# Expert stage: whole 8 KB weight rows, 512-column up products, blocks overlapped on TensorE, at least two blocks an expert

## The chip, the cores and the metric

The kernel runs on one core of a Trainium2 chip. The metric is the device time of one execution in microseconds (us). Engines are called as in the profile: PE (TensorE), DVE (VectorE), ACT (ScalarE), POOL (GpSimd), SP (SyncE, which issues most DMAs).

## The reference, cut to what matters

The program computes a transformer block with a mixer and a mixture of experts, then two further layers, and a last norm, for 512 tokens of width 1024 in float32. The change lies in the mixture of experts: 32 experts, each token goes to 4, and each expert multiplies its tokens by a 1024 x 2048 matrix, applies a gated unit and multiplies by a 1024 x 1024 matrix.

```python
def moe(h, router_w, router_b, w_up, b_up, w_down, b_down):
    logits = (xt @ router_w + router_b).astype(jnp.float32)
    top_vals, top_idx = lax.top_k(logits, TOP_K)
    gates = jax.nn.softmax(top_vals, axis=-1)
    ...
    def expert_block(args):
        e, xb = args
        hu = xb @ w_up[e] + b_up[e]
        g = jnp.minimum(hu[:, :D_FF], SWIGLU_LIMIT)
        lin = jnp.clip(hu[:, D_FF:], -SWIGLU_LIMIT, SWIGLU_LIMIT)
        glu = g * jax.nn.sigmoid(SWIGLU_ALPHA * g)
        return ((lin + 1.0) * glu) @ w_down[e] + b_down[e]
    y_rows = lax.map(expert_block, (blk_expert, x_rows)).reshape(n_rows, d)
    y = jax.ops.segment_sum(y_rows * row_gate[:, None].astype(y_rows.dtype), row_tok, num_segments=t + 1)[:t]
```

## The kernel before, in words

**Blocks.** `route_stages` ranks the token-expert pairs on the device and fills three lists of 97 columns (`MAXB + 1`): which token rows a block takes, where its results go, and its gates. A block is 32 rows (`BR`) of one expert; an expert has its count of rows divided by 32, rounded up, and at least one block. The number of blocks is known only on the device: every engine reads `first_block` and runs its loop over the blocks.

**Rows.** A row of 1024 lies as four pieces of 256 on four groups of 32 partitions (`PARTS`), so a block fills 128 partitions. Since the left operand has 32 columns, four products run beside each other on the four column groups of PE, one for each quarter of the output columns.

**Weights.** An expert has 12 chunks of 1 MB: 8 up chunks, each two DMAs of 512 KB whose contiguous runs are 512 columns (2 KB), and 4 down chunks, one DMA with runs of 1024 columns (4 KB). 21 chunk buffers (`LENT`) are used in turn, a chunk being loaded into the buffer of the one 21 before it, so that SP (line 1832 on) waits for PE to have used that one in the last block of its expert. At most four chunks are in flight (`ahead`). The chunks of expert 0 and four of expert 1 are loaded in the routing stage.

**A block before.** PE (line 1940 on): seven up chunks, the transpose of the first half of the hidden units (line 1917), the eighth up chunk, two down chunks, the transpose of the second half, then the wait for the gather and the transposes of the next block's rows (line 1896), then two down chunks. Up products (line 1909) have 256 columns in two banks, one for each half of the hidden units. DVE adds the bias (2002), clamps (2004, 2005), multiplies (2007, 2009) with ACT's sigmoid (1972); ACT copies the transposes (1974, 1964). When the down products are done, DVE adds the bias (2012) and scales (2017) to give y.

**Gather and scatter.** POOL runs one loop (line 1878): once block b's rows are turned it issues the gather of b+1 (1865, an indirect DMA of 128 pieces of 1 KB) and then, once y is ready, the scatter of b (1873, an indirect DMA that adds y to x in memory). Instructions of one engine stay in their order, so a gather stands behind the scatter ahead of it:

```python
pool.wait_ge(rows_turned, b + 1)
gather(b + 1, b * 2 + 3)
pool.wait_ge(y_stored, b * 16 + 16)
pool.sem_inc(y_free, 1)
scatter(b, b * 2 + 4, b + 2)
```

There is one buffer for the gathered rows, one for y. The biases of an expert come on SP's queue and are spread over the partitions by line 1995.

## Time and profile before

| | |
|---|---|
| median of 3 runs | 3347.1 us (3343.88 to 3348.02) |
| profiled execution, its span | 3352.8 us |
| PE busy | 2825.7 us (84%) |
| DVE, ACT, POOL busy | 1291.4, 898.9, 280.1 us |
| expert stage, first to last product | 588.7 to 1738.5 us |
| bytes moved in the whole program | 581.92 MB |

The span runs from the first to the last instruction. The page cuts it into 40 slices of 83.8 us; PEclk is the clock granted to PE in tenths of 2.4 GHz. A float32 product shows as two records of the profile for each product of the program. A DMA's time to landing runs from its issue to its last semaphore update. SP's 512 KB DMAs share a semaphore, so the profile gives no landing for them.

### The profile page before, as it was taken

The numbers are of one execution on the slowest core, as the hardware profiler recorded it, in microseconds if no ns is written. First come the engines' busy times: TensorE is split into PE (matmuls) and PEld (weight loads), VectorE is DVE, ScalarE is ACT, GpSimd is POOL, SyncE is SP. The second block draws the span as 40 slices with busy tenths as digits, with TensorE's granted clock in tenths as the row PEclk, the third lists the DMA queues.
The fourth block names the chain that finished last, engine by engine and source line by source line (L and its number), as shares of the span: only waits on it lengthen the run. The fifth ranks groups of instructions, "written<-read, shape, count | busy, mean of one in ns | idle before, by whom it ended". The sixth has DMA issues, their size and how long they took to land. (4 is left out here: it accounts for less than half of the span.)

```text
span 3352.8 us, 65854 instructions
## 1 busy us (share of the span) xinstructions
PE 2825.7 (84%) x25476; PEld 2041.8 (61%) x25477; DVE 1291.4 (39%) x2922; ACT 898.9 (27%) x1856; POOL 280.1 (8%) x365
## 2 busy tenths in 40 slices
PE   6987675888888867989969597899999688899998
PEld 4965475444444423545538475778887566778886
DVE  1236554223222212333323474444443365643343
ACT  2233321112121101222213143343332133532232
POOL 1000000122221211222210100000000100000000
PEclk7996676899999967999989698999999788899999
DMA  6243006899999999799972300022221210022221
GB/s 181 77 154 117 1 13 252 318 385 344 382 386 387 344 391 388 241 353 386 361 260 84 96 1 26 26 76 101 101 101 60 69 51 1 26 73 85 95 101 50
DMA packets 299974, 581.92 MB, mean 174 GB/s; under 512 B 35780, under 2 KB 74372, under 8 KB 299764
## 3 DMA queue, kind: packets, MB, share of 16 engines
q1 hardware_dynamic: 279876, 557.27, 45.5%
q0 software_dynamic: 15792, 21.34, 2.9%
q8 instruction: 137, 2.24, 0.3%
q10 hardware_dynamic: 4098, 0.49, 0.1%
q14 instruction: 71, 0.58, 0.1%
HBM read 562.25 MB, written 16.78 MB: 173 GB/s over the span
## 5 line engine op out<-in xcount | busy, mean ns | idle before, releaser
L1909 PE MATMUL moe_up<-expert_w,mod 128*32 128x256 f32 x3856 | 243.1, 397 | 24.1 <-DMA expert_w<-in_exp_w_up 18.2
L1909 PE MATMUL moe_up<-ring,mod 128*32 128x256 f32 x3184 | 200.7, 402 | 30.9 <-issue 19.2
L1972 ACT ACTIVATE mod<-mod 128x128 f32<-128x128 f32 x158 | 48.9, 310 | 637.8 <-DVE mod L2004 637.8
L360 PE MATMUL mlp_bank<-hT_hi,mlp_w 128*128 128x512 f32 x512 | 199.4, 390 | 0.0
L362 PE MATMUL mlp_bank<-hT_hi,mlp_w 128*128 128x512 f32 x512 | 199.2, 389 | 0.0
L361 PE MATMUL mlp_bank<-hT_lo,mlp_w 128*128 128x512 f32 x512 | 199.2, 389 | 0.0
L360 PE MATMUL mlp_bank<-mlp_w,mlp_u_hi 128*128 128x512 f32 x512 | 199.2, 389 | 0.0
L361 PE MATMUL mlp_bank<-mlp_w,mlp_u_hi 128*128 128x512 f32 x512 | 199.2, 389 | 0.0
L362 PE MATMUL mlp_bank<-mlp_w,mlp_u_lo 128*128 128x512 f32 x512 | 199.2, 389 | 0.0
L1909 PEld LDWEIGHTS moe_up<-expert_w,mod 128*32 128x32 f32 x3856 | 122.7, 113 | 120.7 <-issue 27.1
L2002 DVE TENSOR_TENSOR mod<-moe_up,mod 128x256 f32<-128x256 f32 x158 | 67.1, 425 | 320.8 <-PE moe_up L1909 317.6
L402 ACT ACTIVATE mlp_w<-ring 128x1024 fp32r<-128x1024 f32 x128 | 125.1, 1053 | 207.8 <-PE mlp_bank L362 207.8
L1873 POOL DMA_INDIRECT mixed_rows<-mod,moe_place x80 | 128.3, 1604 | 544.2 <-DVE mod L2017 523.1
L1909 PEld LDWEIGHTS moe_up<-ring,mod 128*32 128x32 f32 x3184 | 104.2, 115 | 112.2 <-issue 46.0
L411 DVE TENSOR_TENSOR mlp_w<-ring,mlp_w 128x1024 fp32r<-128x1024 f32 x128 | 148.1, 1220 | 6.4 <-ACT mlp_w L402 6.4
L2012 DVE TENSOR_TENSOR mod<-moe_down,mod 128x256 f32<-128x256 f32 x79 | 33.6, 425 | 283.2 <-PE moe_down L1931 283.2
L1931 PE MATMUL moe_down<-expert_w,mod 128*32 128x256 f32 x2064 | 131.8, 393 | 1.7 <-DMA expert_w<-in_exp_w_down 0.4
L1508 DVE TENSOR_TENSOR x<-x,mlp_bank 128x512 f32<-128x512 f32 x64 | 43.9, 687 | 222.3 <-PE mlp_bank L362 222.3
L2427 DVE TENSOR_TENSOR mlp_relu<-mlp_relu 128x512 f32<-128x512 f32 x64 | 44.2, 691 | 191.2 <-ACT mlp_u_hi L2424 191.2
L360 PEld LDWEIGHTS mlp_bank<-hT_hi,mlp_w 128*128 128x128 f32 x512 | 96.1, 188 | 20.5 <-DVE hT_lo L671 0.4
L362 PEld LDWEIGHTS mlp_bank<-hT_hi,mlp_w 128*128 128x128 f32 x512 | 96.1, 188 | 20.1
L362 PEld LDWEIGHTS mlp_bank<-mlp_w,mlp_u_lo 128*128 128x128 f32 x512 | 96.1, 188 | 20.1
(522 smaller groups left out, 5765.1 us busy)
## 6 DMA issues: line engine op xcount, KB each, us to landing
expert_w<-in_exp_w_up SPq DMA_DIRECT2D x194, 512.0 KB
ring<-in_exp_w_up SPq DMA_DIRECT2D x150, 512.0 KB
ring<-in_w_ff SPq DMA_DIRECT2D x32, 2048.0 KB, 8.7
expert_w<-in_exp_w_down SPq DMA_DIRECT2D x47, 1024.0 KB, 11.1
ring<-in_exp_w_down SPq DMA_DIRECT2D x39, 1024.0 KB, 10.8
moe_w<-in_exp_w_up SPq DMA_DIRECT2D x74, 512.0 KB
ring<-in_ada_w SPq DMA_DIRECT2D x12, 2048.0 KB, 11.9
hT<-in_exp_w_up SPq DMA_DIRECT2D x48, 512.0 KB
```

The source lines that it names most:

```text
L360: nc.tensor.matmul(out, lhsT.hi, rhs.hi, start=(i == 0), stop=False)
L361: nc.tensor.matmul(out, lhsT.hi, rhs.lo, start=False, stop=False)
L362: mm = nc.tensor.matmul(out, lhsT.lo, rhs.hi, start=False, stop=last)
L402: nc.scalar.activation(halves.hi[:, at], w[:, at], ACT.Copy).then_inc(hi_made, 1)
L411: nc.vector.tensor_tensor(halves.lo[:, at], w[:, at], halves.hi[:, at].bitcast(F32), ALU.subtract).then_inc(lo_made, 1)
L1508: return nc.vector.tensor_tensor(k.x[:, t, cols], k.x[:, t, cols], psum, ALU.add)
L1873: pool.indirect_dma_start(x_parts, bass.IndirectOffsetOnAxis(ap=place[:], axis=0), y, None, compute_op=op).then_inc(y_stored, 16)
L1909: mm = nc.tensor.matmul(up[half][quarter[q], 0:2 * UNITS], rowsT[:, f % 2, quarter[f // 2]], chunk[r][c][:, :, j, q * UNITS:(q + 1) * UNIT ...
L1931: mm = nc.tensor.matmul(down[quarter[q], 0:YCOLS], hidT[:, half, quarter[f]], chunk[r][c][:, j, q * YCOLS:(q + 1) * YCOLS], start=(half == ...
L1972: nc.scalar.activation(sig[:, half], pre[:, half, 0:UNITS], ACT.Sigmoid, scale=ALPHA).then_inc(sig_ready, 1)
L2002: nc.vector.tensor_tensor(pre[:, half], up[half][:, 0:2 * UNITS], bias[:, 2 * half * UNITS:2 * (half + 1) * UNITS], ALU.add).then_inc(up_t ...
L2427: chain(nc.vector.tensor_tensor(r, r, r, ALU.mult))
```

## The change

The numbers of the lists become 126 columns (`LISTS`), and every expert has at least two blocks (`FEWEST`). An up chunk holds one group of 128 input rows with all 2048 columns, a down chunk two neighbouring rows on each partition: each chunk is one DMA of 1 MB with runs of 8 KB. The up products of a quarter take both halves of the gated unit at once, 512 columns, in one bank; the hidden units of even and odd number are turned separately, to fit the order of rows in the down chunks. On PE, `both` puts the up products of block b ahead of the down products of block b-1, also across experts. The turns of rows run one block further ahead, the first two gathers are issued ahead of POOL's loop, and DVE's work is split into `hidden` (block b) and `output` (block b-1). The six hidden-unit steps on DVE and ACT are done once a block at twice the width. The bias is spread in two parts (`spread_bias`).

```diff
-MAXB = S * TOPK // BR + NE
-UNITS = COL // PARTS
+FEWEST = 2
+MAXB = S * TOPK // BR + FEWEST * NE - TOPK
+LISTS = MAXB + 2
...
-            chain(nc.vector.tensor_scalar(blocks[:], count[:], 1.0, float(BR - 1), ALU.max, ALU.add))
+            chain(nc.vector.tensor_scalar(blocks[:], count[:], float((FEWEST - 1) * BR + 1), float(BR - 1), ALU.max, ALU.add))
...
 def load_expert_chunk(k, a, sp, e, c, r):
     dst = k.expert_chunk(c, r)
-    if c < 8:
-        half, two = c // 4, c % 4
-        for part in range(2):
-            col = part * FF + half * COL
-            src = a["exp_w_up"][0].rearrange("e (k p) n -> e p k n", p=P)[bass.ds(e, 1), :, 2 * two:2 * two + 2, col:col + COL]
-            sp.dma_start(dst[:, part], src.rearrange("e p k n -> (e p) k n")).then_inc(k.expert_loaded[c], 16)
+    if c < UPS:
+        src = a["exp_w_up"][0].rearrange("e (k p) n -> e p k n", p=P)[bass.ds(e, 1), :, c, :]
+        sp.dma_start(dst, src.rearrange("e p n -> (e p) n")).then_inc(k.expert_loaded[c], 16)
     else:
-        src = a["exp_w_down"][0].rearrange("e (k p) n -> e p k n", p=P)[bass.ds(e, 1), :, 2 * (c - 8):2 * (c - 7), :]
-        sp.dma_start(dst, src.rearrange("e p k n -> (e p) k n")).then_inc(k.expert_loaded[c], 16)
+        src = a["exp_w_down"][0].rearrange("e (q p h) n -> e p q (h n)", p=P, h=2)[bass.ds(e, 1), :, c - UPS, :]
+        sp.dma_start(dst, src.rearrange("e p n -> (e p) n")).then_inc(k.expert_loaded[c], 16)
 def expert_stage(k, a, h2_dram, x_dram):
...
-                last_but_one, last = first_block(sp, e - 1), first_block(sp, e)
+                begin, end = first_block(sp, e - 1), first_block(sp, e)
                 for c in range(c0, CHUNKS):
                     if c == LENT - CHUNKS:
-                        sp.wait_ge(bias_spread, e)
+                        sp.wait_ge(bias_spread, e * 2)
                         load_bias(e)
-                    if c < LENT - CHUNKS:
-                        sp.wait_ge(chunk_done, last_but_one * CHUNKS + (c + 2 * CHUNKS - LENT + 1))
+                    old = (c + CHUNKS - LENT) % CHUNKS
+                    last = begin if c < LENT - CHUNKS else end
+                    if old < UPS:
+                        sp.wait_ge(up_done, last * UPS + (old + 1))
                     else:
-                        sp.wait_ge(chunk_done, last * CHUNKS + (c + CHUNKS - LENT + 1))
+                        sp.wait_ge(down_done, last * DOWNS + (old - UPS + 1))
                     sp.sem_inc(chunk_free, 1)
                     ahead = (c - 4) % CHUNKS
-                    sp.wait_ge(loaded[ahead], e * landed(ahead) + (landed(ahead) if c >= 4 else 0))
+                    sp.wait_ge(loaded[ahead], e * 16 + (16 if c >= 4 else 0))
...
             scatter(MAXB, 2, 1, ALU.bypass)
+            pool.wait_ge(rows_turned, 1)
+            gather(1, 3)
             with pool.Fori(0, first_block(pool, NE)) as b:
-                pool.wait_ge(rows_turned, b + 1)
-                gather(b + 1, b * 2 + 3)
+                pool.wait_ge(rows_turned, b + 2)
+                gather(b + 2, b * 2 + 4)
                 pool.wait_ge(y_stored, b * 16 + 16)
                 pool.sem_inc(y_free, 1)
-                scatter(b, b * 2 + 4, b + 2)
+                scatter(b, b * 2 + 5, b + 2)
...
+            def up_chunk(e, r, c):
+                pe.wait_ge(loaded[c], e * 16 + 16)
+                w = chunk[r][c].rearrange("p (s q n) -> p q s n", s=2, q=PARTS)
+                for q in range(PARTS):
+                    mm = nc.tensor.matmul(up[quarter[q], :], rowsT[:, c % 2, quarter[c // 2]], w[:, q], start=(c == 0), stop=(c == UPS - 1))
+                mm.then_inc(up_done, 1)
+            def turn_hidden(b):
+                pe.wait_ge(hid_ready, b)
+                pe.wait_ge(hid_taken, b)
+                for h in range(2):
+                    tr = nc.tensor.transpose(turn_h[:, h * P:(h + 1) * P], hid_by_unit[:, h, :], k.ident[:])
+                tr.then_inc(hid_turned, 1)
+            def down_chunk(e, r, c):
+                pe.wait_ge(loaded[c], e * 16 + 16)
+                at = c - UPS
+                w = chunk[r][c].rearrange("p (h n) -> p h n", h=2)
+                for h in range(2):
                     for q in range(PARTS):
...
+                        mm = nc.tensor.matmul(down[quarter[q], 0:YCOLS], hidT[:, h, quarter[at]], w[:, h, q * YCOLS:(q + 1) * YCOLS],
+                                              start=(at == 0 and h == 0), stop=(at == DOWNS - 1 and h == 1))
+                mm.then_inc(down_done, 1)
+            def start_up(e, r, b):
+                pe.wait_ge(rows_taken, b + 1)
+                pe.wait_ge(up_taken, b + 1)
+                for c in range(2):
+                    up_chunk(e, r, c)
+            def open_down(e, r, b):
+                pe.wait_ge(hid_taken, b + 1)
+                pe.wait_ge(down_taken, b)
+                for c in range(UPS, UPS + 2):
+                    down_chunk(e, r, c)
+            def both(e, r, b, e_down, r_down):
+                start_up(e, r, b)
+                turn_hidden(b)
+                for c in range(2, UPS):
+                    up_chunk(e, r, c)
+                open_down(e_down, r_down, b)
+                pe.wait_ge(gathered, b * 16 + 32)
+                turn_rows()
+                for c in range(UPS + 2, CHUNKS):
+                    down_chunk(e_down, r_down, c)
+            def rest(e, r):
+                with pe.Fori(first_block(pe, e) + 1, first_block(pe, e + 1)) as b:
+                    both(e, r, b, e, r)
+            def run(e, r):
+                both(e, r % CYCLE, first_block(pe, e), e - 1, (r - 1) % CYCLE)
+                rest(e, r % CYCLE)
+            pe.nop().then_inc(up_done, UPS)
+            pe.nop().then_inc(down_done, DOWNS)
             pe.wait_ge(gathered, 16)
             turn_rows()
...
+            start_up(0, 0, 0)
+            for c in range(2, UPS):
+                up_chunk(0, 0, c)
+            pe.wait_ge(gathered, 32)
+            turn_rows()
+            rest(0, 0)
+            with pe.Fori(0, (NE - 1) // CYCLE) as i:
+                for r in range(1, CYCLE + 1):
                     run(i * CYCLE + r, r)
...
+            for e in range((NE - 1) // CYCLE * CYCLE + 1, NE):
+                run(e, e)
+            blocks = first_block(pe, NE)
+            turn_hidden(blocks)
+            open_down(NE - 1, (NE - 1) % CYCLE, blocks)
+            for c in range(UPS + 2, CHUNKS):
+                down_chunk(NE - 1, (NE - 1) % CYCLE, c)
...
+            def take_hidden(b):
+                act.wait_ge(hid_turned, b)
+                nc.scalar.activation(hidT, turn_h[:, 0:2 * P].rearrange("p (h n) -> p h n", n=P), ACT.Copy).then_inc(hid_taken, 1)
+            def open_gate(b):
+                act.wait_ge(gate_ready, b + 1)
+                nc.scalar.activation(sig, gate, ACT.Sigmoid, scale=ALPHA).then_inc(sig_ready, 1)
+                act.wait_ge(rows_turned, b + 2)
+                take_rows()
...
+            def hidden(b):
+                dve.wait_ge(up_done, b * UPS + 2 * UPS)
+                nc.vector.tensor_tensor(pre, up[:], bias_up, ALU.add).then_inc(up_taken, 1)
+                dve.wait_ge(up_taken, b + 2)
+                nc.vector.tensor_scalar(gate, gate, LIMIT, None, ALU.min).then_inc(gate_ready, 1)
+                nc.vector.tensor_scalar(lin, lin, LIMIT, -LIMIT, ALU.min, ALU.max).then_inc(step, 1)
+                dve.wait_ge(sig_ready, b + 1)
+                nc.vector.tensor_tensor(gate, gate, sig, ALU.mult).then_inc(step, 1)
+                dve.wait_ge(step, b * 2 + 2)
+                nc.vector.scalar_tensor_tensor(hid, lin, 1.0, gate, ALU.add, ALU.mult).then_inc(hid_ready, 1)
+            def output(b):
+                dve.wait_ge(y_ready, b)
+                dve.sem_inc(bias_seen, 1)
+                dve.wait_ge(down_done, b * DOWNS + DOWNS)
+                nc.vector.tensor_tensor(whole, down[:, 0:YCOLS], bias_down, ALU.add).then_inc(down_taken, 1)
+                dve.wait_ge(down_taken, b + 1)
+                dve.wait_ge(y_free, b)
+                nc.vector.scalar_tensor_tensor(y, whole, k.row_gate[:, bass.ds(b, 1)], out_scale, ALU.mult, ALU.mult).then_inc(y_ready, 1)
```

The body of PE's loop over blocks in expert 0 before (`moe_up` and `moe_down` are the banks of the two products, `ring` and `expert_w` weight buffers, `mod` the rows and hidden units):

```order
L1909 MATMUL moe_up<-ring,mod 32x256 x32
L1904 REGISTER_ALU
L1909 MATMUL moe_up<-ring,mod 32x256 x16
L1909 MATMUL moe_up<-expert_w,mod 32x256 x8
L1917 MATMUL moe_turn_hid<-ident,mod 128x128
L1909 MATMUL moe_up<-expert_w,mod 32x256 x8
L1925 REGISTER_ALU
L1926 ISA
L1931 MATMUL moe_down<-expert_w,mod 32x256 x16
L1917 MATMUL moe_turn_hid<-ident,mod 128x128
L1950 ISA
L1896 MATMUL moe_turn_rows<-ident,mod 128x128 x2
L1925 REGISTER_ALU
L1931 MATMUL moe_down<-expert_w,mod 32x256 x16
```

And now, the loop over the second and further blocks of expert 0:

```order
L1901 MATMUL moe_up<-ring,mod 32x512 x8
L1909 MATMUL moe_turn_hid<-ident,mod 128x128 x2
L1901 MATMUL moe_up<-ring,mod 32x512 x16
L1901 MATMUL moe_up<-expert_w,mod 32x512 x8
L1918 MATMUL moe_down<-expert_w,mod 32x256 x16
L1943 ISA
L1894 MATMUL moe_turn_rows<-ident,mod 128x128 x2
L1918 MATMUL moe_down<-expert_w,mod 32x256 x16
```

The transposes of hidden units are together behind the first two up chunks; the down products behind the up products are those of the block before. The turn of rows has two down chunks behind it in both.

POOL's loop before, from the copy of the gather's indices to the scatter:

```order
L1862 ISA
L1862 COPY moe_index<-row_token 128x1
L1863 ISA
L1865 DMA mod<-h_rows,moe_index 128x256
L1883 ISA
L1869 ISA
L1869 COPY moe_place<-row_place 128x1
L1870 REGISTER_ALU
L1871 REGISTER_ALU
L1873 DMA mixed_rows<-mod,moe_place 2560x256
```

And now:

```order
L1858 ISA
L1858 COPY moe_index<-row_token 128x1
L1859 ISA
L1861 DMA mod<-h_rows,moe_index 128x256
L1881 ISA
L1865 ISA
L1865 COPY moe_place<-row_place 128x1
L1866 REGISTER_ALU
L1869 DMA mixed_rows<-mod,moe_place 2560x256
```

The gather still stands ahead of the scatter in the loop, and one of each is issued a round; only the block numbers and the wait's count differ.

## Rows read from the trace of the kernel before

**Rows 1.** The page, 40 slices of the span: mean busy share of 16 DMA engines, tenths.

```profile
DMA  6243006899999999799972300022221210022221
```

**Rows 2.** The stage (PE first), then line 2012 alone; last columns PEclk, DMA share, GB/s.

```profile
588.70:1738.50 1149.80, 975.25 (x15484) 522.81 (x15484) 320.05 (x1008) 222.68 (x474) 234.31 (x314) 0.93 0.98 355
...
1187.00:1220.20 33.20, 0.42 (x1) 0.64 1.05 392
1253.20:1286.10 32.90, 0.42 (x1) 0.60 1.05 390
1371.80:1434.10 62.30, 2.12 (x5) 1.00 0.68 232
1480.00:1700.00 220.00, 7.22 (x17) 1.00 1.03 376
```

**Rows 3.** Timeline of a block: start us, us, engine, line, [idle before].

```profile
1584.78 0.44 PE L1896 MATMUL moe_turn_rows<-ident,mod 128*128 128x128 f32 x2
...
1587.71 0.48 DVE L2017 SCALAR_TENSOR_TENSOR mod<-mod,row_gate 128x256 f32<-128x256 f32 x1
1589.01 1.61 POOL L1873 DMA_INDIRECT mixed_rows<-mod,moe_place  x1 [4.50 <-DVE mod L2017]
...
1591.63 1.00 POOL L1865 DMA_INDIRECT mod<-h_rows,moe_index  x1 [0.81 <-POOL moe_index L1862]
...
1597.29 0.20 PEld L1896 LDWEIGHTS moe_turn_rows<-ident,mod 128*128 128x128 f32 x2 [0.96 <-DMA mod<-h_rows,moe_index]
...
1495.73 0.44 PE L1896 MATMUL moe_turn_rows<-ident,mod 128*128 128x128 f32 x2 [0.90 <-DMA mod<-h_rows,moe_index]
...
1736.13 0.38 PE L1896 MATMUL moe_turn_rows<-ident,mod 128*128 128x128 f32 x2
```

**Rows 4.** Timeline, a block whose gather is early.

```profile
599.85 0.38 PE L1896 MATMUL moe_turn_rows<-ident,mod 128*128 128x128 f32 x2
...
602.13 5.36 PE L1909 MATMUL moe_up<-ring,mod 128*32 128x256 f32 x96
...
605.83 0.42 DVE L2002 TENSOR_TENSOR mod<-moe_up,mod 128x256 f32<-128x256 f32 x1 [2.40 <-PE moe_up L1909]
...
607.22 0.29 DVE L2009 SCALAR_TENSOR_TENSOR mod<-mod 128x128 f32<-128x128 f32 x1
...
611.42 0.14 PEld L1917 LDWEIGHTS moe_turn_hid<-ident,mod 128*128 128x128 f32 x1 [0.56 <-DVE mod L2009]
...
611.59 0.38 PE L1896 MATMUL moe_turn_rows<-ident,mod 128*128 128x128 f32 x2
```

**Rows 5.** The page, a 128x512 add.

```profile
L1508 DVE TENSOR_TENSOR x<-x,mlp_bank 128x512 f32<-128x512 f32 x64 | 43.9, 687 | 222.3 <-PE mlp_bank L362 222.3
```

**Rows 6.** Queues in 1196:1204 (up), 1219:1228 (down): packets, MB, rate.

```profile
DMA packets 1605, 3.09 MB, mean 387 GB/s; under 512 B 94, under 2 KB 94, under 8 KB 1605
...
DMA packets 1034, 3.66 MB, mean 406 GB/s; under 512 B 59, under 2 KB 59, under 8 KB 1034
```

**Rows 7.** Queues in 1204:1212: packets, MB, share of 16 engines.

```profile
q0 software_dynamic: 192, 0.26, 14.3%
```

**Rows 8.** Queues in 1409:1420 (idle), 1589:1598 (2 KB), 1601:1611 (4 KB); us to landing.

```profile
mixed_rows<-mod,moe_place POOLq DMA_INDIRECT x1, 3.8
mod<-h_rows,moe_index POOLq DMA_INDIRECT x1, 2.9
...
mixed_rows<-mod,moe_place POOLq DMA_INDIRECT x1, 6.9
mod<-h_rows,moe_index POOLq DMA_INDIRECT x1, 5.6
...
mixed_rows<-mod,moe_place POOLq DMA_INDIRECT x1, 8.5
mod<-h_rows,moe_index POOLq DMA_INDIRECT x1, 6.7
```

**Rows 9.** Queues in the whole stage, 588:1740; last number: median us to landing.

```profile
mod<-h_rows,moe_index POOLq DMA_INDIRECT x79, 5.8
```

More of the change, by code:

```diff
@@ L1669, in _ @@
                 pe.wait_ge(rows_ready, 2 * n + 2)
[L1670 removed]
+                mm = nc.tensor.matmul(t_bank[:, 0:LISTS], row_hot[:, n, :], blk_hot[:, n, :], start=(n == 0), stop=(n == NT * TOPK - 1))
             mm.then_inc(lists_ready, 1)
@@ L1897, in turn_rows @@
                 tr.then_inc(rows_turned, 1)
-            def up_chunk(e, r, b, c):
-                half, two = c // 4, c % 4
-                pe.wait_ge(loaded[c], e * landed(c) + landed(c))
-                if two == 0:
-                    pe.wait_ge(up_taken, b * 2 + (half + 1))
-                for j in range(2):
-                    f = 2 * two + j
-                    for q in range(PARTS):
-                        mm = nc.tensor.matmul(up[half][quarter[q], 0:2 * UNITS], rowsT[:, f % 2, quarter[f // 2]],
-                                              chunk[r][c][:, :, j, q * UNITS:(q + 1) * UNITS], start=(f == 0), stop=(f == ND - 1))
-                mm.then_inc(chunk_done, 1)
@@ L1913, in turn_hidden @@
-            def turn_hidden(b, half):
-                pe.wait_ge(hid_ready, b * 2 + (half + 1))
-                pe.wait_ge(hid_taken, b * 2 + (half + 1))
-                nc.tensor.transpose(turn_h[half][:, 0:P], hid[:, half, :], k.ident[:]).then_inc(hid_turned, 1)
-            def down_chunk(e, r, b, c):
-                half, two = (c - 8) // 2, c % 2
-                if c == 8:
-                    pe.wait_ge(y_ready, b + 1)
-                if two == 0:
-                    pe.wait_ge(hid_taken, b * 2 + (half + 3))
-                pe.wait_ge(loaded[c], e * landed(c) + landed(c))
-                for j in range(2):
-                    f = 2 * two + j
-                    for q in range(PARTS):
-                        mm = nc.tensor.matmul(down[quarter[q], 0:YCOLS], hidT[:, half, quarter[f]], chunk[r][c][:, j, q * YCOLS:(q + 1) * YCOLS],
-                                              start=(half == 0 and f == 0), stop=(half == 1 and f == 3))
-                mm.then_inc(chunk_done, 1)
@@ L1955, in _ @@
-            with pe.Fori(0, NE // CYCLE) as i:
-                for r in range(CYCLE):
-                    run(i * CYCLE + r, r)
-            for r in range(NE % CYCLE):
-                run(NE // CYCLE * CYCLE + r, r)
+            start_up(0, 0, 0)
[6 more added lines that the diff above has]
+                for r in range(1, CYCLE + 1):
+                    run(i * CYCLE + r, r)
@@ L1967, in _ @@
+            act.nop().then_inc(hid_taken, 1)
             act.wait_ge(rows_turned, 1)
             take_rows()
-            with act.Fori(0, first_block(act, NE)) as b:
-                for half in range(2):
-                    act.wait_ge(gate_ready, b * 2 + (half + 1))
-                    nc.scalar.activation(sig[:, half], pre[:, half, 0:UNITS], ACT.Sigmoid, scale=ALPHA).then_inc(sig_ready, 1)
-                    act.wait_ge(hid_turned, b * 2 + (half + 1))
-                    nc.scalar.activation(hidT[:, half, :], turn_h[half][:, 0:P], ACT.Copy).then_inc(hid_taken, 1)
-                act.wait_ge(rows_turned, b + 2)
-                take_rows()
+            open_gate(0)
@@ L2020, in reload_stage @@
+            open_expert(0)
+            hidden(0)
+            spread_bias(bias_down, bias_row[:, UPW:], 0, 1)
+            rest(0)
+            with dve.Fori(1, NE) as e:
+                begin = first_block(dve, e)
+                open_expert(e)
+                hidden(begin)
+                output(begin)
+                spread_bias(bias_down, bias_row[:, UPW:], e, 1)
+                rest(e)
+            output(first_block(dve, NE))
 def reload_stage(k, x_dram):
```

132 lines of the change are left out of this document (51 added, 81 removed).

## Prediction

> **What bounds the kernel now.** I read first the strip of 40 slices, to find where the change lives [rows 1]: the products of the expert stage (lines 1909 and 1931) run from 588.7 to 1738.5 us, and there the line of the DMA engines says 9 in most slices. Two suspects, so the next view is the table by stretches [rows 2]. Over the stage the DMA share is 0.98 at 355 GB/s; PE is busy 975 of 1149.8 us, and a busy PE is not yet a PE that decides. The table restricted to line 2012 (one per block of 32 rows) shows what an expert costs: the first and the last of three neighbours with one block take 33.2 and 32.9 us, the queues at 1.05, PEclk 0.64 and 0.60. There the transfers decide. With five blocks it takes 62.3 us, the queues at 0.68: there something per block decides. I counted the blocks of all 32 experts in this way: six experts have one block, ten two, twelve three, three four, one five, 79 together.
>
> What decides a block is in the timeline of one [rows 3]. PE's transposes of the gathered rows (line 1896) start at 1584.78; two down chunks and the bias add follow, y is ready at 1588.19 (1587.71 + 0.48), GpSimd starts the scatter-add of y at 1589.01, then the gather of the next rows at 1591.63, and the next transposes start at 1597.29, having waited 0.96 us for that gather. 3.41 + 0.82 + 2.62 + 5.66 = 12.51 us: a closed loop, since GpSimd issues the gather behind the scatter in program order and the scatter waits for y. Between the transposes at 1495.73 and 1736.13 lie 19 blocks, 12.65 us each. PE alone needs less: where the gather is early (turns at 599.85 and 611.59, [rows 4]) a block takes 11.7 us.
>
> **What the new order does to that loop.** Nothing, and this is what the forecast rests on. In the new PE order the down products of block b-1 stand behind the up products of block b, and the rows of b+1 are turned before the last two down chunks. Those two chunks, the add, the scatter of y(b-1) and then the gather of rows b+2 follow each other exactly as before; the gather is numbered two ahead, but the pipeline is one block deeper, and in GpSimd's loop it still stands behind the scatter of the block whose down products have just ended. Each link keeps its instructions: the 16 down products of two chunks, the 128x256 add and scaling, the same two indirect DMAs. Hidden units in other order, 512-column add, sigmoid, clamps: these lie on DVE and ACT and start two down chunks ahead of the turn of rows. At half the width the steps take 1.7 us from the first add at 605.83 to the end of the last product at 607.51 [rows 4]; twice the width at most doubles this (a 128x512 add takes 0.69 us [rows 5], a 128x256 one 0.42), and from the end of the up products to the loop's add there are two down chunks, the turn and two down chunks, 32 x 2 records of 55.8 ns and 0.4, 4 us. Cost nothing; without that cover at most 3.4 us in the loop.
>
> On PE the up products halve in number and double in width. 96 records of 256 columns take 5.36 us in rows 4, 55.8 ns each, and 128 of them 7.1 us; 64 of 512 columns the same 7.1 at equal column rate (the other bound: if part of the 55.8 ns is issue, up to 1 us a block less). The wait for the hidden units goes (0.56 us at 611.42, rows 4). So PE needs 11.1 instead of 11.7 us, but the loop needs 12.5: the 0.6 us become a longer wait for the gather. The gain from pipelining is zero while the queues are loaded.
>
> **Transfers.** A stretch with only up chunks (packets of 2 KB) moves 387 GB/s; one with down chunks almost alone (4 KB) 406 GB/s [rows 6]. Per packet and engine that is 84.7 and 161.4 ns, so 76.7 ns for each 2 KB and 8.0 for a packet; for 8 KB I estimate 315 ns, 416 GB/s. Bounds: 406 if nothing comes past 4 KB, 427 if the 8.0 goes entirely. An expert has 8.39 MB up and 4.19 MB down: 21.7 + 10.3 = 32.0 us before, 30.2 after (29.5 to 31.0). A block's gather and scatter add 192 packets with 14.3% of 8 us = 1.14 us [rows 7], and 32.0 + 1.14 is the 33 measured. The Trainium skill, "DMA: Bandwidth & Descriptors", under "Rules for kernel authors", asks for 1 MiB or more a DMA for bandwidth; the up chunks had 512 KB and now have it, but its reason, a fixed cost each, is hidden here by four chunks in flight, and the sum gains from it only through the rate above.
>
> **The price of 8 KB packets.** A gather beside idle queues lands after 2.9 us, its scatter after 3.8; beside 2 KB packets 5.6 and 6.9; beside 4 KB packets 6.7 and 8.5 [rows 8]. The median of the gathers of the stage is 5.8 [rows 9]. So larger weight packets delay GpSimd's small ones. With 128 rows on 16 engines, each engine has 8 packets of the scatter-add, then the gather behind them; if every small one lets one weight packet pass, going from 4 to 8 KB adds 8 x 153 ns = 1.2 us, and a little for the gather's own. The lone pair 5.6 and 6.7 gives 0.55 us per KB, 8.9 at 8 KB; the lowest end is 5.6, if only bytes count. I take 7.1, 1.3 us more than now, nearest to the counted packets: loop 12.65 + 1.3 = 13.95 us. The skill's same page ("Queues, rings and completion order") says that an engine goes round its queues packet by packet; that agrees with these landings and speaks against this change.
>
> **Two blocks or more.** The six experts with one block get a second: 85 blocks. Beside the transfers each costs 1.14 us there (its 14 us of PE work fit into 32); in total 7 us, less where PE catches up. The routing lists grow from 97 to 126 columns on some 50 short VectorE instructions ahead of the stage; 256 columns more cost 0.27 us by the two adds just named, 29 columns then 0.03 us: +1.5 us, not hidden.
>
> **The sum.** For each expert I take the longer of transfers T and loop L. Before: T = 32.0 + 1.14n, L = 12.65n, so 33.1, 34.3, 38.0, 50.6, 63.3 us for one to five blocks, 1212 over the counts above. The stage has 1150: 16 of 384 chunks are loaded ahead (some 43 us), and nine chunks of lookahead let neighbours help each other. So only differences are used. After: T = 30.2 + 1.14n, L = 13.95n: sixteen experts at 32.5, twelve at 41.9, three at 55.8, one at 69.8: 1260, +48. Against it: transfers then fill less of the stage (85 x 1.14 + 30.7 x 30.2 = 1024 us of nearly 1190), so some tenth of the gathers find idle queues and win about 2.3 us each (13.95 down to what PE needs with its waits), some -17. With the lists, +33 us: 3352.8 + 33 = 3386 for the profiled execution; its span is 5.7 us above the median of the runs, so 3347.1 + 33 = 3380.
>
> **Rivals.**
> *The landing does not grow.* If the engines change queues after so many bytes and not after a packet, the gather stays at 5.8 and the loop at 12.65. For it: the median lies much nearer to the 2 KB case than to the single 6.7, though a third of the bytes come in 4 KB packets. Against it: rows 8. Then T sinks, L stays: 16 x 32.5 + 455 + 152 + 63 = 1190 against 1212, -22; if neighbours share the transfers' gain better, 85 x 12.65 = 1075 and the stalls of the five thin experts, down to -50. Time 3347 - 35 = 3312. The skill has a rule of this effect: the page named above, "SWDGE vs HWDGE vs iDMA", gives a packet as preferably 4096 B at most, the boundary at which an engine changes queues; were the 8 KB runs cut so, the landing would be that beside 4 KB at most. The point from which the sign turns is a landing of about 6.5 us.
> *They cancel.* Landing near 6.5: within 0.2% (6.7 us), which is about what a measurement can tell from no change. 3347.
> *The clock falls.* The wait at the turn of rows grows from about 1 to 3 us a block. In the thin experts, where PE waits again and again, PEclk is 0.60 (the lower level, 1.2 GHz, most of the time), in 1480 to 1700 us it is 1.00 [rows 2]. If the longer wait lets it fall in half of the 53 blocks of the thick experts and each then loses 4 us at half speed, +106 us more: 3486. Against it: each wait follows 11 us of dense products.
> *The DMAs are not 8 KB.* If the transfers show 2 or 4 KB packets, the change keeps T and only the blocks count: +2 to +8.
>
> **Chances.** Forecast 0.52; landing unchanged, with the gain, 0.34; cancelling or short packets 0.09; clock 0.05. Its own range is +10 to +70, 3357 to 3417. For 8 in 10 the range must take in most of the rival: 3302 to 3410. Faster 0.35, same 0.08, slower 0.57.
>
> **What would show it.** In the new profile: 64 up records a block (up products near 112 ns each in a full stretch); 85 adds of down products; transfers near 416 GB/s in thin stretches, thin experts at about 32.5 us; the gather landing at 7 us or more and the scatter at 9 to 10; the distance of two turns of rows near 14 us where three or more blocks follow each other, with 2 us or more of PE waiting for the gather. A landing under 6.5 makes the forecast wrong by its decisive step; a distance below 12 us would say that the loop is not what I take it for.

## The result, and the profile after

| | before | changed |
|---|---|---|
| median of 4 runs | 3346.2 us (3343.9 to 3348.0) | 3439.0 us (3437.7 to 3444.5) |
| profiled span | 3352.8 us | 3436.8 us |
| turns of rows, first and last | 586.30, 1736.13 (80) | 587.14, 1822.47 (86) |

The changed kernel is slower: ratio 1.0281, 95% interval 1.0266 to 1.0296, +93 us. The forecast was 3380 (+33) and its range ended at 3410, so the direction was right and the size wrong. Between the first and the last turn of rows (PE's transposes of a block's gathered rows) lie 1149.8 us before and 1235.3 after: 85.5 us, and the two profiled spans differ by 84.0. So the whole difference lies in this stage; the 93 us of the medians are more because the profiled execution of the kernel before was 6.6 us above the median of its runs.

The page's strip of the DMA engines, which answers to [rows 1]:

```profile
DMA  6242007897999799688883210022222210012221
```

The table by stretches, whole stage first, then one thin expert (two blocks) and the stretch of [rows 2], with line 2026 (one add a block) in place of 2012; last columns PEclk, DMA share, GB/s:

```profile
588.30:1822.50 1234.20, 1033.92 (x11121) 393.86 (x11121) 282.88 (x716) 100.95 (x254) 249.81 (x336) 0.94 0.86 332
...
1170.90:1203.10 32.20, 0.85 (x2) 0.95 0.84 326
1480.00:1700.00 220.00, 6.36 (x15) 0.95 0.90 349
```

The share of the DMA engines has gone from 0.98 to 0.86. Stretches with full queues read 1.03 to 1.05 [rows 2], so before they were nearly full over the stage; now they are idle for a seventh of it or more, in the thin experts (one or two blocks of rows) too: 0.84, where three neighbours with one block had 1.05. In the same 220 us there are 15 blocks for 17.

The waits of PE in the stage (us in total, times, longest), first the two largest waits for a DMA in the kernel before, where the waits for up chunks take some 37 us together:

```profile
PE moe_turn_rows L1896 <- DMA mod<-h_rows,moe_index: 49.6, 55, 2.3
...
PE moe_up L1909 <- DMA expert_w<-in_exp_w_up: 25.7, 17, 7.0
```

And in the changed kernel:

```profile
PE moe_turn_rows L1894 <- DMA mod<-h_rows,moe_index: 178.6, 70, 3.8
PE moe_up L1901 <- issue: 16.4, 21, 5.8
PE moe_up L1901 <- DMA ring<-in_exp_w_up: 3.8, 1, 3.8
```

The wait for a chunk of weights is almost gone; the wait for the gathered rows has more than tripled. The queues of the stage, and the landings of the gather (5.8 in [rows 9]) and of the scatter:

```profile
DMA packets 69762, 409.74 MB, mean 332 GB/s; under 512 B 8840, under 2 KB 19836, under 8 KB 22560
...
q1 hardware_dynamic: 53612, 386.28, 77.2%
...
mod<-h_rows,moe_index POOLq DMA_INDIRECT x85, 7.3
mixed_rows<-mod,moe_place POOLq DMA_INDIRECT x83, 8.8
```

69,762 - 22,560 = 47,202 packets have 8 KB or more, which the 368 weight chunks of the stage need at 128 rows of 8 KB each (47,104): the weights do travel in packets of 8 KB. Two blocks in the timeline, as in [rows 3]: the first at full clock, the second not.

```profile
1638.33 0.44 PE L1894 MATMUL moe_turn_rows<-ident,mod 128*128 128x128 f32 x2 [2.78 <-DMA mod<-h_rows,moe_index]
1638.69 1.93 PE L1918 MATMUL moe_down<-expert_w,mod 128*32 128x256 f32 x32
...
1641.25 0.48 DVE L2029 SCALAR_TENSOR_TENSOR mod<-mod,row_gate 128x256 f32<-128x256 f32 x1
...
1642.55 1.60 POOL L1869 DMA_INDIRECT mixed_rows<-mod,moe_place  x1 [5.15 <-DVE mod L2029]
...
1645.14 0.99 POOL L1861 DMA_INDIRECT mod<-h_rows,moe_index  x1 [0.80 <-POOL moe_index L1858]
...
1653.45 0.44 PE L1894 MATMUL moe_turn_rows<-ident,mod 128*128 128x128 f32 x2 [3.65 <-DMA mod<-h_rows,moe_index]
1653.82 3.36 PE L1918 MATMUL moe_down<-expert_w,mod 128*32 128x256 f32 x32
...
1657.78 0.48 DVE L2029 SCALAR_TENSOR_TENSOR mod<-mod,row_gate 128x256 f32<-128x256 f32 x1
...
1661.67 0.99 POOL L1861 DMA_INDIRECT mod<-h_rows,moe_index  x1 [0.80 <-POOL moe_index L1858]
...
1669.12 0.44 PE L1894 MATMUL moe_turn_rows<-ident,mod 128*128 128x128 f32 x2 [2.52 <-DMA mod<-h_rows,moe_index]
```

It is the loop of the prediction: turn, two down chunks, y (3.40 us after the turn), scatter (+0.82), gather (+2.59), next turn, 8.31 us later here. In the second block the same 32 records of down products take 3.36 us for 1.93, and y comes 4.81 us after the turn. The granted clock in the two legs was:

```profile
1639.00:1642.40 3.40, 3.40 (x49) 1.33 (x42) 0.91 (x2) 0.18 (x1) 0.00 (x0) 1.00 1.00 424
1653.40:1656.80 3.40, 3.35 (x34) 1.79 (x38) 0.00 (x0) 0.38 (x1) 0.00 (x0) 0.61 0.80 335
```

Taken over all blocks of the timeline, turn to turn (median): 12.87 us before, 14.64 after; from the gather's issue to the next turn 5.84 and 7.39. The leg from the turn to y is over 3.8 us, a "long leg", in 31 of 83 blocks (8 of 78 before).

### The profile page after: what moved, and what is told of

Read it like the earlier page. It is cut to its first block and busy times, and to the rows that moved or that the text cites. A ratio compares the mean times of both kernels' runs of the same rounds, so it can differ in the third digit from the quotient of the medians.

```text
span 3436.8 us, 55529 instructions
## 1 busy us (share of the span) xinstructions
PE 2887.0 (84%) x21212; PEld 1911.5 (56%) x21213; DVE 1255.6 (37%) x2633; ACT 777.0 (23%) x1638; POOL 297.8 (9%) x391
## 5 line engine op out<-in xcount | busy, mean ns | idle before, releaser
L1901 PE MATMUL moe_up<-expert_w,mod 128*32 128x512 f32 x2040 | 244.7, 614 | 17.0 <-issue 13.2
L2012 DVE TENSOR_TENSOR mod<-moe_up,mod 128x512 f32<-128x512 f32 x85 | 58.8, 691 | 523.9 <-PE moe_up L1901 523.9
L1901 PE MATMUL moe_up<-ring,mod 128*32 128x512 f32 x1696 | 204.6, 613 | 3.5 <-ACT mod L1980 2.0
L1894 PE MATMUL moe_turn_rows<-ident,mod 128*128 128x128 f32 x172 | 39.2, 311 | 186.0 <-DMA mod<-h_rows,moe_index 185.9
L1901 PEld LDWEIGHTS moe_up<-expert_w,mod 128*32 128x32 f32 x2040 | 66.1, 114 | 157.1 <-issue 145.4
L1989 ACT ACTIVATE mod<-mod 128x256 f32<-128x256 f32 x85 | 35.4, 417 | 512.3 <-DVE mod L2014 512.3
L412 DVE TENSOR_TENSOR mlp_w<-ring,mlp_w 128x1024 fp32r<-128x1024 f32 x128 | 148.1, 1219 | 6.1 <-ACT mlp_w L403 6.1
L1918 PE MATMUL moe_down<-expert_w,mod 128*32 128x256 f32 x2176 | 147.8, 413 | 0.0
L1894 PEld LDWEIGHTS moe_turn_rows<-ident,mod 128*128 128x128 f32 x172 | 17.8, 145 | 226.5 <-DMA mod<-h_rows,moe_index 220.7
L1985 ACT ACTIVATE mod<-moe_turn_hid 128x256 f32<-128x256 f32 x85 | 32.6, 383 | 388.5 <-PE moe_turn_hid L1909 384.4
L1901 PEld LDWEIGHTS moe_up<-ring,mod 128*32 128x32 f32 x1696 | 54.0, 114 | 113.9 <-issue 104.1
```

The costliest lines, as they stand in the source:

```text
L412: nc.vector.tensor_tensor(halves.lo[:, at], w[:, at], halves.hi[:, at].bitcast(F32), ALU.subtract).then_inc(lo_made, 1)
L1894: tr = nc.tensor.transpose(turn_r[:, j * P:(j + 1) * P], rows[:, j * P:(j + 1) * P], k.ident[:])
L1901: mm = nc.tensor.matmul(up[quarter[q], :], rowsT[:, c % 2, quarter[c // 2]], w[:, q], start=(c == 0), stop=(c == UPS - 1))
L1918: mm = nc.tensor.matmul(down[quarter[q], 0:YCOLS], hidT[:, h, quarter[at]], w[:, h, q * YCOLS:(q + 1) * YCOLS], start=(at == 0 and h == 0) ...
L2012: nc.vector.tensor_tensor(pre, up[:], bias_up, ALU.add).then_inc(up_taken, 1)
```

## The experiments

The landing, the distance of turns ("turns", median and mean) and the number of long y legs are read from each run's own trace. "Us" is the median; the ratio is to the kernel before on the same chip, with its interval. A blank means that the trace does not tell it, or that the run has no leg of that kind to compare.

| run | us | ratio | landing | turns | long legs | DMA share |
|---|---|---|---|---|---|---|
| before | 3346 | 1 | 5.8 | 12.87, 14.55 | 8 | 0.98 |
| changed | 3439 | 1.0281 (1.0266-1.0296) | 7.3 | 14.64, 14.53 | 31 | 0.86 |
| e1_runs_4k | 3375 | 1.0087 (1.0070-1.0104) | 6.3 | 13.40, 13.78 | 13 | 0.94 |
| e2_early_gather | 3264 | 0.9749 (0.9733-0.9766) | | 11.61, 12.47 | | 0.98 |
| e3_before_early | 3327 | 0.9935 (0.9919-0.9952) | | 11.74, 14.30 | | 0.99 |
| e4_before_two | 3355 | 1.0019 (1.0009-1.0029) | | 12.73, 13.59 | 4 | 0.98 |
| e5_turn_late | 3314 | 0.9894 (0.9877-0.9910) | 7.6 | 12.51, 13.08 | | 0.94 |
| e6_runs_2k | 3381 | 1.0093 (1.0076-1.0110) | 5.7 | 12.68, 13.85 | 8 | 0.99 |
| e7_early_runs_4k | 3294 | 0.9834 (0.9817-0.9850) | | 11.84, 12.80 | | 1.00 |
| e8_filled_wait | 3447 | 1.0298 (1.0281-1.0315) | 7.4 | 14.63, 14.59 | 24 | 0.86 |
| e9_packets_before | 3360 | 1.0043 (1.0026-1.0059) | 5.8 | 12.69, 13.65 | 5 | 0.98 |
| e10_long_fill | 3448 | 1.0299 (1.0281-1.0316) | 7.7 | 14.55, 14.71 | 0 | 0.85 |
| e11_after_three | 3615 | 1.080 (1.073-1.087) | 7.0 | 14.16, 14.02 | 34 | 0.78 |
| e12_before_three | 3516 | 1.0505 (1.0475-1.0536) | 5.9 | 12.89, 13.04 | 2 | 0.88 |

### The packets: e1_runs_4k, e6_runs_2k, e9_packets_before

```diff
+    run = 2 * D // SPLIT                    # e1: SPLIT = 2, e6: SPLIT = 4
+    for part in range(SPLIT):
+        sp.dma_start(dst[:, part * run:(part + 1) * run], flat[:, part * run:(part + 1) * run]).then_inc(k.expert_loaded[c], 16)
```

```diff
+        if c < UPS:                         # e9: SPLIT = 2, runs of 2 KB for the up chunks
+            d, f = (t.rearrange("p (s t n) -> p s t n", s=2, t=2)[:, :, part, :] for t in (dst, flat))
```

> The changed kernel with each 1 MB chunk loaded by two DMAs of 4 KB runs instead of one of 8 KB; PE order, columns, block counts as in the change. Theory L (the time is 85 turns of a loop turn-of-rows, two down chunks, y, scatter, gather; 8 KB packets lengthen it by delaying the gather): the gather's landing falls from 7.3 to about 6.1 us, the turn-to-turn distance from 14.6 to 13.2 to 13.4, the program from 3439 to 3330 to 3350 us, although the transfers get slower. Rival B (the overlap on PE and the six more blocks are what costs, packets do not matter): landing may move, the program stays within 3420 to 3440 us.

> The changed kernel with every 1 MB chunk fetched by four DMAs whose packets have 2 KB; order, products and blocks as changed. PACKET THEORY (the packet size of the weights, by the landing of the gather and the clock drop that follows the longer wait, is the whole loss): landing 5.8 us, turns 12.7 to 12.9 us apart where blocks follow each other, 85 x 12.8 = 1088 us is less than what the transfers need, so the DMA engines decide again: stage 1150 to 1165 us as in the kernel before with two blocks an expert, time 3350 to 3365, below the run with 4 KB packets (3375). RIVAL (a part of the loss is the new order itself or the 512-column products): stays at 3375 or above, with turns 13.3 us or more apart at a landing of 5.8.

> The changed kernel with the packets of the kernel before: up chunks in two DMAs of 512 KB whose packets have 2 KB, down chunks in two DMAs of 512 KB with packets of 4 KB; order, 512-column products and blocks as changed. The run with 2 KB everywhere came to 3381 with turns 12.7 us apart, but its transfers moved only 380 GB/s, so the transfers of the down chunks and the smaller DMAs, not the order, should have held it. PACKET THEORY: 387 and 406 GB/s again, gather landing 5.8 to 6.0 us, stage 1150 to 1165 us, 3348 to 3364, like the kernel before with two blocks an expert (3355). RIVAL (new order or 512-column products cost by themselves): 3372 or more.

Order, products and blocks are those of the changed kernel in all three. Queues over the stage of e1, e6 and e9: the rate, then the gather's median landing.

```profile
DMA packets 122791, 409.96 MB, mean 350 GB/s; under 512 B 14728, under 2 KB 25724, under 8 KB 122684
...
mod<-h_rows,moe_index POOLq DMA_INDIRECT x85, 6.3
```

```profile
DMA packets 228791, 410.13 MB, mean 348 GB/s; under 512 B 26504, under 2 KB 37500, under 8 KB 228668
...
mod<-h_rows,moe_index POOLq DMA_INDIRECT x85, 5.7
```

```profile
DMA packets 185254, 409.94 MB, mean 353 GB/s; under 512 B 14728, under 2 KB 25724, under 8 KB 185148
...
mod<-h_rows,moe_index POOLq DMA_INDIRECT x85, 5.8
```

The landing follows the size of the weight packets, 5.7, 6.3 and 7.3 us beside 2, 4 and 8 KB, and with it the distance of the turns: 12.68, 13.40 and 14.64. The size of the DMAs changes along with that of the packets (256 KB, 512 KB, 1 MB), but e9, with DMAs of 512 KB like e1 and smaller packets in two thirds of the bytes, lands at 5.8 for 6.3. e1 ended 25 us above its range although the median distance of its turns, 13.40, is the one expected: the mean is 13.78, and part of the blocks wait for weights (26 us in total for up chunks). e6 ended 16 above its range, at the turns expected; its transfers move about 380 GB/s in full slices, and e9, which differs in the packets and DMAs alone and has 387 there, took 21 us less. e9 bears on the rest. With the packets of before the new order and the 512-column products run in 3360 us, inside its range and within 5 us of e4, the old order with as many blocks. At 85 blocks the packets, with the DMA size that goes with them, are worth 3439 - 3360 = 79 us.

### The blocks: e4_before_two, e11_after_three, e12_before_three

```diff
-            chain(nc.vector.tensor_scalar(blocks[:], count[:], 1.0, float(BR - 1), ALU.max, ALU.add))
+            chain(nc.vector.tensor_scalar(blocks[:], count[:], float(BR + 1), float(BR - 1), ALU.max, ALU.add))
```

e11 and e12 have `2 * BR + 1` there, the changed kernel and the kernel before. In e4 and e12 the lists grow to 125 columns, and a scratch tile of the routing stage takes another's memory to make room.

> The kernel before with at least two blocks an expert (85 instead of 79, lists of 125 columns), all else as before. My term for this part: +7 us for the traffic of six blocks in experts that wait for transfers, +1.5 for the lists: 3353 to 3356 us. Rival: each block costs a turn of the loop, 6 x 12.65 = 76 us: 3420 us.

> The changed kernel with three blocks or more an expert: the six experts with one block of rows and the ten with two get three, 101 blocks for 85 (the added ones hold no token). SUM THEORY (the stage takes the longer of the transfers of all experts and the loops of all blocks, because the weights read ahead carry slack from expert to expert; in the changed kernel that is the loops, everywhere): 16 x 14.6 = 233 us more than the changed kernel's 3439, 3650 to 3700. PER-EXPERT THEORY (the prediction's sum: each expert takes the longer of its own transfers and its own loops): sixteen experts go from 32.5 to 41.9 us, +150, 3589.

> The kernel before with three blocks or more an expert, 101 blocks. With two or more (85 blocks) it took 3355, 9 us more than with 79. SUM THEORY: with 85 blocks the transfers decide (1155 us against 85 x 12.75 = 1084 of loops); with 101 the loops, 101 x 12.75 = 1288 us, overtake the transfers (1155 + 18), so the stage grows by 133 us where six blocks had cost 5: 3470 to 3505, turns 12.7 to 12.8 us apart on the mean, the DMA share below 0.92. PER-EXPERT THEORY: sixteen experts go from 34.3 to 38.0 us, +59, 3414.

In the old kernel six more blocks cost 6.6 us against the kernel before on the same chip (3354.9 for 3348.2); 5 us of the stage in the profiled executions (1149.8 to 1154.7). Sixteen more on top cost 161 us, 10 a block. Its stage in e12 (PE, PEld, DVE, ACT, POOL busy, then PEclk, DMA share, GB/s):

```profile
586.00:1903.00 1317.00, 1190.68 (x19764) 662.28 (x19764) 401.74 (x1274) 285.65 (x605) 301.12 (x404) 0.99 0.88 314
```

The DMA share fell to 0.88. The turns are 13.04 us apart on the mean (12.75 expected). So blocks are nearly free as long as the transfers decide, and cost 10 us as soon as the loops do. From one spreading of the bias (line 1995, once an expert) to the next, experts with two blocks of rows take 28.4 us on the mean in e4, five of nine under 27 (two loops) and not the 34.3 of their own transfers; with three blocks, in e12, 38.7. The sum over the whole stage was much nearer (+133 expected for the stage, +59 by experts, +162 measured; the time 11 us above the range). For the changed kernel e11 went against it: +176 us, with an uncertainty of some 23 from two runs, where the sum over the stage said +233 and the sum by experts +150. The loops got shorter there, 14.02 us for 14.53 on the mean; 38 of 99 gathers reached the next turn within 6.5 us, against 16 of 83, perhaps because with fewer bytes a block more of them found idle queues. What holds in both is the price: 10 to 11 us a block where the loops decide.

### The place of the gather: e2_early_gather, e3_before_early, e5_turn_late, e7_early_runs_4k

```diff
             gather(1, 3)
-            with pool.Fori(0, first_block(pool, NE)) as b:
-                pool.wait_ge(rows_turned, b + 2)
-                gather(b + 2, b * 2 + 4)
+            pool.wait_ge(rows_turned, 2)
+            gather(2, 4)
+            with pool.Fori(0, first_block(pool, NE) - 1) as b:
+                pool.wait_ge(rows_turned, b + 3)
+                gather(b + 3, b * 2 + 5)
```

Left out here: the last scatter follows behind the loop. e3 is the same edit, one number lower, in the kernel before, with lists one column longer; e7 is e2 with the two DMAs of 4 KB runs of e1. e5 leaves POOL alone and moves two lines of PE:

```diff
-                pe.wait_ge(gathered, b * 16 + 32)
-                turn_rows()
                 for c in range(UPS + 2, CHUNKS):
                     down_chunk(e_down, r_down, c)
+                pe.wait_ge(gathered, b * 16 + 32)
+                turn_rows()
```

> The changed kernel with POOL issuing every gather one block earlier, ahead of the scatter that it stood behind: the loop is opened, packets stay at 8 KB. Theory L: PE no longer waits for the gather, turns of rows 11.4 us apart where weights are there, 32 us an expert where not; stage 1241 to about 1050 us, program near 3250 us. Rival T (the stage is bound by transfers or by PE at the lower clock, and the gather wait only fills their time): under 30 us gained, 3410 us or more.

> The kernel before with the same opening of the loop (gathers one block earlier; lists one column longer), all else as before. Theory L: blocks 11.7 instead of 12.65 us apart where the loop set them; by the longer of 32.0 + 1.14n and 11.7n for each expert 1165 against 1212 us, so 3346 - 47 = 3300 us. Rival T: the stage before was bound by transfers nearly everywhere, under 10 us gained.

> The changed kernel with one move in the PE order: the wait for the gathered rows and their two transposes stand behind the last two down chunks of block b-1, not ahead of them. The scatter of y(b-1) and the gather behind it are then issued about 3 us ahead of the point in PE's order at which the turn now stands, and the gather has the up products of a whole block to land in. LOOP THEORY (gather issued behind y, rows turned before the last down chunks, is what decides every block): the loop opens, turns 11.4 to 12.5 us apart, the DMA engines at 0.97 or more again, stage about 1060 to 1090 us, time 3255 to 3300, near the run with the early gather (3264). RIVAL (the early gather won by putting the gather ahead of the scatter on GpSimd's queue, or by landing beside other packets): order on GpSimd is unchanged here, so 3400 or more.

> The changed kernel with every gather one block early (3264 by itself) and its chunks in two DMAs of 4 KB packets. LOOP THEORY: the landing of the gather no longer counts, only the transfers do; 4 KB packets cost 161 ns where 8 KB cost 309, so 4 per cent more at most for the weights: 406 for 410 to 416 GB/s, stage +5 to +25 us, time 3268 to 3290. RIVAL (even with the early gather the landings beside 8 KB packets cost time): faster than 3258.

In e2 the gather goes out right behind the turn and ahead of the scatter:

```profile
1541.13 0.44 PE L1900 MATMUL moe_turn_rows<-ident,mod 128*128 128x128 f32 x2
...
1542.78 1.00 POOL L1861 DMA_INDIRECT mod<-h_rows,moe_index  x1 [0.80 <-POOL moe_index L1858]
1544.66 0.48 DVE L2035 SCALAR_TENSOR_TENSOR mod<-mod,row_gate 128x256 f32<-128x256 f32 x1
1545.97 1.60 POOL L1869 DMA_INDIRECT mixed_rows<-mod,moe_place  x1 [2.00 <-DVE mod L2035]
```

Its stage, and PE's longest waits in it:

```profile
585.00:1645.00 1060.00, 1000.98 (x11122) 374.61 (x11122) 283.68 (x718) 101.59 (x255) 253.30 (x337) 0.97 0.98 387
```

```profile
PE moe_up L1907 <- issue: 24.3, 29, 6.0
PE moe_up L1907 <- DMA ring<-in_exp_w_up: 17.8, 13, 2.1
```

No wait for the gather is left, the DMA share is 0.98 again, and the 8 KB packets move 387 GB/s over the stage where before moved 355: 3264 us, 175 below the changed kernel and 82 below the kernel before. e3 shows the same edit where the transfers decide nearly everywhere: 21 us, where the changed kernel gains 175, and fewer than the 47 expected; its DMA share is 0.99. So 21 of the 82 us come with the early gather alone, and 63 lie between e3 and e2, which also differ in order and blocks. e7 is 30 us slower than e2, 4 over its range: with the gather out of the loop the larger packets are the better ones, by 30 us over 4 KB; 2 KB beside an early gather was not run.

e5 opens the same loop from PE's side, with POOL's order untouched; its rival is out, since it gains 125 us. It ended 14 us above its range, for the turn has nothing behind it to cover ACT's copy of the transposed rows:

```profile
1493.45 0.44 PE L1894 MATMUL moe_turn_rows<-ident,mod 128*128 128x128 f32 x2
...
1493.92 0.38 ACT L1980 ACTIVATE mod<-moe_turn_rows 128x256 f32<-128x256 f32 x1 [2.47 <-PE moe_turn_rows L1894]
...
1494.62 1.92 PE L1901 MATMUL moe_up<-moe_w,mod 128*32 128x512 f32 x16 [0.73 <-ACT mod L1980]
```

Over the stage that wait came to 58.7 us in 78 times, and the one for the gather to 14.1.

### The clock: e8_filled_wait, e10_long_fill

```diff
                 open_down(e_down, r_down, b)
+                for _ in range(6):          # e10: 18
+                    nc.tensor.transpose(turn_r[:, 3 * P:4 * P], k.ident[:], k.ident[:])
                 pe.wait_ge(gathered, b * 16 + 32)
```

> The changed kernel with six transposes of the identity (about 1.9 us) into an unread part of the bank, put ahead of PE's wait for the gathered rows; all results as before. It leaves the gather where it is and takes only idleness of PE away. CLOCK THEORY (the two down chunks behind the wait run at half clock in 31 of 83 blocks because PE had idled 2.5 to 3.6 us just before): y is ready 3.4 us after the turn in nearly all blocks, 31 x 1.3 = 40 us less, minus what the filler costs where the gather is early: time 3400 to 3420. RIVAL (the clock falls in a rhythm of its own, or because PE is busy too long): 3435 or more, the long legs as many as before.

> The changed kernel with 18 transposes of the identity ahead of PE's wait for the gathered rows. Six took 0.87 us together and left 1.9 us of idleness a block; 18 take 2.6 us, so PE should idle under 0.5 us there in most blocks. CLOCK BY IDLENESS: the two down chunks behind the wait run at full clock in nearly all blocks (y 3.4 us after the turn), 10 long legs or fewer of 83, and 3405 to 3430. RIVAL (idleness ahead of the wait is not what lowers the clock): 25 long legs or more, 3440 to 3465, since the filler delays the blocks whose gather is early.

In the changed kernel PE had waited 3.04 us on the mean ahead of the 31 long legs, 1.59 ahead of the 53 others. e8 was too weak to tell: its six transposes took 0.87 us, not the 1.9 I had reckoned, and 24 legs stayed long. In e10, with 18, PE waited 0.70 us on the mean, and none of 83 legs was long; one leg of it:

```profile
1598.74 2.19 PE L1944 MATMUL moe_turn_rows<-ident 128*128 128x128 f32 x18
1601.99 0.44 PE L1894 MATMUL moe_turn_rows<-ident,mod 128*128 128x128 f32 x2 [1.06 <-DMA mod<-h_rows,moe_index]
1602.36 1.93 PE L1918 MATMUL moe_down<-hT,mod 128*32 128x256 f32 x32
```

So the clock falls to its lower level (1.2 GHz) behind PE's wait, as the rival had it, and with the wait filled it no longer does. The time did not follow: 3448. The mean y leg lost 0.5 us, but from the gather's issue to the turn it was 7.93 us for 7.28. About 0.46 of this lies between the landing and the turn, for the filler also stands in front of turns whose rows were there (no turn came within 6.5 us any more, where 16 had), and the rest in a later landing. My expectation of 3405 to 3430 forgot the first; why the landing is later no run shows. That the clock is worth net time is therefore not shown. Inside the changed kernel the 28 long blocks under 17.5 us take 15.47 us, the 42 others of over 12.6 us take 14.44: 28 x 1.03 = 29 us, an estimate from the trace that hangs on these two limits, which I chose.

## Why the prediction was right and wrong

**Right: the loop decides, and the new order does not change it.** Its three fixed legs read 3.41, 0.81 and 2.60 us (medians) after the change, and e9's turns are 12.69 us apart against 12.73 in e4. PE needed 11.40 us in blocks whose gather was early (11.1 foreseen), and 48 records of up products of 512 columns in a row took 5.36 us in e5, 112 ns each, as foreseen. That the loop decides is shown by e2 and e5, which open it in two ways and gain 175 and 125 us.

**Right in kind, 0.2 us short: the landing.** I took 7.1 us, it is 7.3. The scatter (9 to 10 foreseen) is 8.8. The rule that was weighed against the change holds: the Trainium skill, "DMA: Bandwidth & Descriptors", "Queues, rings and completion order", lets an engine change queues only packet by packet, and the landings of 5.7, 6.3 and 7.3 us agree. Whether a packet of that rule is a packet of the profile no run here shows. The rival drawn from the Trainium skill, same page, "SWDGE vs HWDGE vs iDMA", packets cut at 4096 B, did not come: the profile counts 47,202 packets of 8 KB or more. Transfers moved about 410 GB/s in the full slices of the stage; I had 416 for thin experts.

**Wrong: the reason against the clock.** I gave this rival 0.05, since each wait follows 11 us of dense products. The clock falls all the same, in 31 of 83 blocks, and costs 1.3 us a leg, not 4. The legs are longer by it, but by e10 it is open whether the time is.

**Wrong, and the largest: the sum.** The step that failed is "So only differences are used". "For each expert I take the longer of transfers T and loop L" gave 1212 us for a stage that measures 1150, and I took that error for one that stays the same. It did not. The same rule gave 1260 - 17 = 1243 us for the changed stage, and 1235.3 were measured. So the sum was 62 us too high before and 8 after, and these 54 us are what is missing from the stage: 31 foreseen, 85.5 measured.

The traces show where. Taken from the start of one expert's bias spreading on DVE (line 1995 before, the first of two at line 2006 after) to the next, and for the last expert to the end of its y, in us (thin experts have one or two blocks of rows):

| | sum before | measured | sum after | measured |
|---|---|---|---|---|
| 16 thin experts | 542 | 454 | 520 | 483 |
| 16 thick experts | 671 | 699 | 740 | 761 |

The sum had the thin experts gain 22 us and the thick ones lose 69, or 52 with the credit of 17; they lost 29 and 62. So the error is mainly in the thin experts. What the sum priced wrong is a thin expert's T. In the kernel before, the nine chunks read ahead carry a thick expert's spare transfer time to the thin ones behind it, so that most of these were done before their own 32.0 + 1.14n us had passed. Three of the six one-block experts took 21.6, 22.4 and 25.1 us; only the three that follow each other took their 33. In the changed kernel a thin expert takes two loops, 30 us, and the loops had grown: the spare time was used up. That its sum came so near to 1235 is luck in part, for thin experts were put 37 us too high there and thick ones 21 too low.

The whole-stage sums do not give the stage before either. By my own numbers all transfers are 1114 us, some 1071 without the chunks loaded ahead, and all loops 79 x 12.65 = 999, and neither is 1150: the queues are not full in every stretch (0.68 in the expert with five blocks, [rows 2]). What exactly makes up the 1150 stays open.

**Mis-sized: the loop.** I had 13.95 us. Where the gather took over 6.5 us to the next turn, in 69 of 85 distances, they were 14.97 us on the mean: the long legs add 0.49 to the mean leg from the turn to y (3.90 for 3.41, the clock), and the rest is mostly the way from the gather to the turn. The other 16 took 12.66, and the mean of all is 14.53.

**Wrong in its price: two blocks or more.** "In total 7 us": 6.6 in the old kernel (e4), as foreseen. But there the transfers decide. Where the loops do, a block costs 10 to 11 us (e11, e12). How much of the 79 us of the packets would be left with 79 blocks was not measured; the two parts are not independent, and 93 = 7 (blocks) + 7 (order, hardly above the uncertainty) + 79 (packets), each run against the kernel before on its own chip, holds in this sequence only.

**Right in kind: the credit.** I had 17 us for a tenth of the gathers that find idle queues. It was a fifth (16 of 83 turned within 6.5 us of the gather's issue), at 2.3 us less than the others each, some 37 us. It was too small, and the longer loop of the others outweighed it.

## What to carry to other kernels

Before changing the size of a transfer, look for a small transfer in a dependent loop that shares its queues: what the large one gains in rate, the small one pays in latency, and the fix is to issue the small one earlier (here one block, 175 us), not to shrink the large one. A model that does not give back the measured time of the kernel before has found something: its error is to be explained, not cancelled. Here it was transfer time that thin experts borrow from thick ones by reading ahead; such spare time is used up when the loops grow, and a block that was nearly free then costs 10 us. A wait can also lengthen what comes behind it, when PE's clock falls behind it.

## What the runs showed of the hardware

The weight of a packet: a gather of 128 pieces lands after 5.7, 6.3 and 7.3 us beside weight packets of 2, 4 and 8 KB (e6, e1 and the changed kernel, in DMAs of 256 KB, 512 KB and 1 MB; 5.8 in e9, with 2 and 4 KB in DMAs of 512 KB). The rate of the full slices was about 380 GB/s with 2 KB packets in DMAs of 256 KB (387 in DMAs of 512 KB), 400 with 4 KB, and 410 with 8 KB. Six 128x128 transposes of a resident tile took 0.87 us back to back and 18 took 2.19, 0.12 to 0.15 each, where a pair of them standing alone shows 0.44. And the lower clock came in single legs: 1.00 granted in one, 0.61 in the next, behind a wait of 3.65 us; none of 83 legs had it in e10, with the wait filled.
